# Stick-breaking attention issued one head ahead, and a vector-by-matrix product moved from VectorE to TensorE in four column groups

## The reference, cut to what matters

```python
def stick_breaking_attention(q, k, v):          # per head h of 8, dh = 64
    z = einsum('qd,kd->qk', q, k) * 64 ** -0.5
    neg_log_1m_beta = where(mask, softplus(z), 0.0)
    tail = cumsum(neg_log_1m_beta, reverse=True) - neg_log_1m_beta
    a = where(mask, exp(log_sigmoid(z) - tail), 0.0)
    return einsum('qk,kd->qd', a, v)

proj = rms_norm(x, g) @ w_in      # q k v | c_b c_c c_u | g_a g_b, 5120 columns
branch_a = stick_breaking_attention(q, k, v) @ w_sb
branch_b = short_conv_mixer(c_b, c_c, c_u, conv_w) @ w_conv
merged = sigmoid(g_a) * branch_a + sigmoid(g_b) * branch_b
x = x + merged @ w_out            # then router, experts, block two

# block two, needed there only
mod   = silu(c)     @ ada_w + ada_b     # ada_w is 1024 x 6144
mod_c = silu(c_ctx) @ ada_w + ada_b
```

## Time and profile before

| | us |
|---|---|
| median of 3 runs | 3600.28 (3599.87 to 3601.12) |
| the profiled execution, its own time | 3600.31 |
| its span | 3598.5 |
| the stretch of the list, from the first score matmul to the first matmul of the output projection | 130.0 to 528.4 |

### The profile page before, as it was taken

The page is one execution under the profiler, slowest core; times in us unless marked ns, Lnnn a source line. Parts: engine busy times, 40 slices in busy tenths (PEclk is TensorE's granted clock), DMA queues, the critical chain, the costliest instruction groups (busy, mean ns, idle before and its releaser), DMA issues.

```text
span 3598.5 us, 31608 instructions
## 1 busy us (share of the span) xinstructions
PE 3301.9 (92%) x12644; PEld 2110.6 (59%) x12644; DVE 1756.1 (49%) x3055; ACT 1020.0 (28%) x1262; POOL 271.8 (8%) x99
## 2 busy tenths in 40 slices
PE   7899887799977899999979999899999999999998
PEld 3344434444443344444448888677777777777776
DVE  2355482222214433233224888777635555555565
ACT  3524201121103210244023333455532222222222
POOL 0000000000000000000001433232300000000000
PEclk9999998799987999999989999999999999999999
DMA  5123252599970110110022333345454444444451
GB/s 188 47 100 110 95 186 72 201 341 364 366 284 5 47 47 0 70 47 24 24 86 102 131 133 141 135 182 199 179 202 152 152 152 152 144 148 142 174 187 47
DMA packets 270574, 500.01 MB, mean 139 GB/s; under 512 B 10103, under 2 KB 151543, under 8 KB 256920
## 3 DMA queue, kind: packets, MB, share of 16 engines
q1 hardware_dynamic: 239008, 391.67, 31.9%
q10 hardware_dynamic: 24648, 81.64, 5.6%
q0 software_dynamic: 6768, 24.64, 1.8%
HBM read 414.55 MB, written 83.36 MB: 138 GB/s over the span
## 4 chain that ended last, share of the span: by engine, by line
PE 77%; DVE 9%; ACT 8%; issue 4%; DMA 1%; ACTq 0%; DVEq 0%; POOL 0%; SPq 0%
PE P L1907 7%; PE P L1909 7%; PE P L1908 7%; PE P L1487 6%; PE P L1615 6%; PE P L1978 4%; PE P L1980 4%; PE P L1979 4%; PE P L1851 3%; PE P L1564 3%; PE P L1647 3%; PE P L1787 2%; DVE gin L402 2%; PE P L1537 2%; ACT part L1369 2%
## 5 line engine op out<-in xcount | busy, mean ns | idle before, releaser
L1907 PE MATMUL P<-hr,part 128*128 128x512 f32 x1152 | 459.4, 399 | 19.4 <-DVE part L402 19.4
L1908 PE MATMUL P<-hr,part 128*128 128x512 f32 x1152 | 456.0, 396 | 0.0
L1909 PE MATMUL P<-hr,part 128*128 128x512 f32 x1152 | 455.8, 396 | 0.0
L1978 PE MATMUL P<-ge,part 128*128 128x512 f32 x1024 | 402.4, 393 | 49.4 <-DVE y L402 45.5
L1980 PE MATMUL P<-ge,part 128*128 128x512 f32 x1024 | 400.5, 391 | 0.0
L1979 PE MATMUL P<-ge,part 128*128 128x512 f32 x1024 | 400.4, 391 | 0.0
L2026 POOL TENSOR_TENSOR part<-raw,part 128x2048 fp32r<-128x2048 f32 x48 | 230.1, 4795 | 1325.4 <-ACT part L1369 1325.4
L1369 ACT ACTIVATE part<-raw 128x2048 fp32r<-128x2048 f32 x136 | 260.2, 1914 | 190.3 <-PE P L1980 166.9
L402 DVE TENSOR_TENSOR part<-raw,part 128x2048 fp32r<-128x2048 f32 x88 | 201.5, 2291 | 154.5 <-ACT part L1369 154.5
L1487 PE MATMUL P<-H,W 128*128 128x512 f32 x576 | 256.4, 601 | 6.5 <-DVE H L410 6.5
L1907 PEld LDWEIGHTS P<-hr,part 128*128 128x128 f32 x1152 | 217.1, 188 | 71.0 <-DVE part L402 20.2
(11 more groups left out here) (258 smaller groups left out, 4040.7 us busy)
## 6 DMA issues: line engine op xcount, KB each, us to landing
raw<-in_u SPq DMA_DIRECT2D x64, 1024.0 KB, 4.9
raw<-in_v SPq DMA_DIRECT2D x64, 1024.0 KB, 5.3
W<-in_w_in SPq DMA_DIRECT2D x18, 2048.0 KB, 10.1
W<-in_w_gate SPq DMA_DIRECT2D x32, 1024.0 KB, 8.1
W<-in_w_up SPq DMA_DIRECT2D x32, 1024.0 KB, 12.6
W<-in_w_down SPq DMA_DIRECT2D x32, 1024.0 KB, 12.1
w_scratch<-window ACTq DMA_DIRECT2D x16, 2048.0 KB, 7.2
wr<-w_scratch SPq DMA_DIRECT2D x32, 1024.0 KB, 7.2
```

The source lines that it names most:

```text
L1907: t.matmul(bank[f % 3], wh[:, k, js], HR[0][:, k, :], start=k == 0, stop=False)
L1908: t.matmul(bank[f % 3], wh[:, k, js], HR[1][:, k, :], start=False, stop=False)
L1909: ins = t.matmul(bank[f % 3], wl[:, k, js], HR[0][:, k, :], start=False, stop=k == 7)
L1978: t.matmul(b, wh[:, k, js], gh[:, k, :], start=k == 0, stop=False)
```

## The change

Two edits, both to the list and to what its entries do.

**The order of the attention.** Phase 0 of head `h+1` is now issued ahead of phases 1 and 2 of head `h`. The rest (`pj 12..31` and the `ada` entries) is spread evenly between the 24 attention entries. The semaphore values, which were computed as `9 * h + ...`, now come from tables (`AX0`, `AA0`, `AV0`).

**The product with `ada_w`.** It has 13 entries instead of 49, and TensorE does the multiplying. The silu of both vectors is written into `SCP`, a 128x256 tile of zeros in which each group of 32 columns carries the two vectors in its first two columns. Entry `ada n` (n < 12) issues eight matmuls with a 128x32 stationary operand from `SCP` and a 128x512 part of `ada_w` as the moving one; part k goes to partitions 32*(k%4) to 32*(k%4)+31 of bank 6. ScalarE copies bank 6 to `ADR` (one 128x512 copy, part of the next `ada` entry), and four matmuls of 128x128 by 128x2 (against `SEL`, a pattern that picks rows 0 and 1 of every group of 32 and sums the groups) lay the result down in bank 7. VectorE has no part in any of this; after the list it adds the bias from bank 7 in one instruction. The `mg` steps have no `ada` entry between them any more.

```diff
+        SCP, SEL, ADR = ft[0][:, 0:256], ft[0][:, 256:288], ft[1]
...
-        att_steps = [("att", h, ph) for h in range(8) for ph in range(3)]
-        cv_steps = [("pj", p) for p in range(12, 32)]
-        both = []
-        while att_steps or cv_steps:
-            both += att_steps[:1] + cv_steps[:1]
-            del att_steps[:1], cv_steps[:1]
-        ada_steps = [("ada", i) for i in range(49)]
-        ORDER1 = interleave(both, ada_steps, 0.55)
-        ORDER1 += interleave([("pj", p) for p in range(32, 40)], ada_steps, 1)
-        ORDER1 += interleave([("mg", n) for n in range(16)], ada_steps, 1)
-        ORDER1 += ada_steps
+        att_steps = [("att", 0, 0)]
+        for h in range(8):
+            att_steps += ([("att", h + 1, 0)] if h < 7 else []) + [("att", h, 1), ("att", h, 2)]
+        beside = interleave([("pj", p) for p in range(12, 32)], [("ada", i) for i in range(13)], 0.6)
+        last_ada = [x for x in [("ada", i) for i in range(13)] if x not in beside]
+        ORDER1 = interleave(att_steps, beside, len(beside) / 23.0)
+        ORDER1 += beside
+        ORDER1 += interleave([("pj", p) for p in range(32, 40)], last_ada, 1)
+        ORDER1 += [("mg", n) for n in range(16)]
...
-            if kind == "ada" and i < 48 and i % 4 == 0:
-                slots.take(("ada", i // 4))
-            if kind == "ada" and i < 48 and i % 4 == 3:
-                slots.drop(("ada", i // 4), s["ada_v"], 10 * (i // 2) + 8)
+            if kind == "ada" and i < 12:
+                slots.take(("ada", i))
+                slots.drop(("ada", i), s["ada_mm"], max(1, 2 * i))
...
+            v.memset(SCP, 0.0).then_inc(s["z_v"], 1)
+            v.tensor_reduce(out=SEL, in_=ident.rearrange("p (g e) -> p e g", e=32), axis=AX.X, op=ADD).then_inc(s["z_v"], 1)
...
-            dve.wait_ge(s["ada_v"], 240)
-            tt(MOD, MOD, par("ab").unsqueeze(2).broadcast_to([128, 48, 2]), ADD).then_inc(s["ada_v"], 1)
+            dve.wait_ge(s["ada_mm"], 24)
+            tt(MOD, bank[7][:, 0:96].rearrange("p (k n) -> p k n", n=2), par("ab").unsqueeze(2).broadcast_to([128, 48, 2]), ADD).then_inc(s["ada_v"], 1)
...
+            act.wait_ge(s["z_v"], 2)
+            a.activation(SCP.rearrange("p (k n) -> p k n", n=32)[:, :, 0:2], par("cc").rearrange("p (k n) -> p k n", n=2), ACT.Silu).then_inc(s["sc_a"], 1)
             for kind, *i in ORDER1:
                 if kind == "att":
                     attention(*i)
+                elif kind == "ada" and i[0]:
+                    act.wait_ge(s["ada_mm"], 2 * i[0] - 1)
+                    a.activation(ADR, bank[6], ACT.Copy).then_inc(s["ada_a"], 1)
...
             def modulation(n):
-                if n and n % 2 == 0:
-                    u = n // 2 - 1
-                    pe.wait_ge(s["ada_v"], 10 * u + 8)
-                    t.matmul(bank[6], ones, ft[u % 2], start=True, stop=True).then_inc(s["ada_mm"], 1)
+                if n < 12:
+                    w = k8(slot["ada", n])
+                    pe.wait_ge(*full["ada", n])
+                    pe.wait_ge(s["sc_a"], 1)
+                    pe.wait_ge(s["ada_a"], n)
+                    for k in range(8):
+                        lo = 32 * (k % 4)
+                        ins = t.matmul(bank[6][lo:lo + 32, :], SCP[:, 32 * k:32 * k + 32], w[:, k, :], start=k < 4, stop=k >= 4)
+                    ins.then_inc(s["ada_mm"], 1)
+                if n:
+                    pe.wait_ge(s["z_v"], 3)
+                    pe.wait_ge(s["nv"], 33)
+                    pe.wait_ge(s["ada_a"], n)
+                    for c in range(4):
+                        at = 8 * (n - 1) + 2 * c
+                        ins = t.matmul(bank[7][:, at:at + 2], ADR[:, c * 128:(c + 1) * 128], SEL[:, 0:2], start=True, stop=True)
+                    ins.then_inc(s["ada_mm"], 1)
```

More of the change, by code:

```diff
@@ L207, in program @@
         H2 = tiles(38, 8)
-        att_steps = [("att", h, ph) for h in range(8) for ph in range(3)]
-        cv_steps = [("pj", p) for p in range(12, 32)]
-        both = []
-        while att_steps or cv_steps:
-            both += att_steps[:1] + cv_steps[:1]
-            del att_steps[:1], cv_steps[:1]
-        ada_steps = [("ada", i) for i in range(49)]
-        ORDER1 = interleave(both, ada_steps, 0.55)
-        ORDER1 += interleave([("pj", p) for p in range(32, 40)], ada_steps, 1)
-        ORDER1 += interleave([("mg", n) for n in range(16)], ada_steps, 1)
-        ORDER1 += ada_steps
+        att_steps = [("att", 0, 0)]
[7 more added lines that the diff above has]
+        ORDER1 += [("mg", n) for n in range(16)]
+        AX0, AA0, AV0, att_x = {}, {}, {}, []
+        na, nv_ = 0, 0
+        for _, h, ph in att_steps:
+            AX0[h, ph], AA0[h, ph], AV0[h, ph] = len(att_x), na, nv_
+            att_x += [(h, ph, i) for i in range(4 if ph < 2 else 1)]
+            na += (7, 1, 1)[ph]
+            nv_ += (5, 8, 0)[ph]
         pj_evac, n_act = [], 0
@@ L448, in attention @@
                         z = Z[:, OFF[i]:OFF[i] + n]
-                        b = bank[2 + (9 * h + 4 + i) % 4]
-                        dve.wait_ge(s["att_mm"], 9 * h + 5 + i)
+                        x = AX0[h, 1] + i
+                        b = bank[2 + x % 4]
+                        dve.wait_ge(s["att_mm"], x + 1)
                         tt(z, z, b[:, 0:n], SUB).then_inc(s["att_v"], 1)
-                        dve.wait_ge(s["att_v"], 13 * h + 6 + 2 * i)
+                        dve.wait_ge(s["att_v"], AV0[h, 1] + 2 * i + 1)
                         tt(z[:, 0:128], z[:, 0:128], cst("nmask"), ADD).then_inc(s["att_v"], 1)
@@ L468, in conv @@
                 tt(y, y, CB[:, c, :], MUL).then_inc(s["cv"], 1)
-            eye = ident.unsqueeze(1).broadcast_to([128, 4, 128])
-            def modulation(n):
-                if n and n % 2 == 0:
-                    u = n // 2 - 1
[L475 to L495, removed]
             def merge(n, ga, gb, mm, done, gates):
@@ L1151, in attention @@
                         n = 512 - 128 * i
[L1152 removed]
+                        x = AX0[h, 0] + i
+                        act.wait_ge(s["att_mm"], x + 1)
                         if h >= 2:
[L1154 to L1156 removed]
+                            act.wait_ge(s["att_mm"], AX0[h - 2, 2] + 1)
+                        a.activation(Z[:, OFF[i]:OFF[i] + n], bank[2 + x % 4][:, 0:n], ACT.Copy, scale=0.125).then_inc(s["att_a"], 1)
+                    act.wait_ge(s["att_a"], AA0[h, 0] + 4)
                     a.activation(E, Z, ACT.Abs).then_inc(s["att_a"], 1)
[L1158 removed]
+                    act.wait_ge(s["att_a"], AA0[h, 0] + 5)
                     a.activation(E, E, ACT.Exp, scale=-1.0).then_inc(s["att_a"], 1)
[L1160 removed]
+                    act.wait_ge(s["att_a"], AA0[h, 0] + 6)
                     a.activation(E, E, ACT.Ln, bias=1.0).then_inc(s["att_a"], 1)
                 if ph == 1:
[L1163 removed]
+                    act.wait_ge(s["att_v"], AV0[h, 1] + 8)
                     a.activation(Z, Z, ACT.Exp).then_inc(s["att_a"], 1)
                 if ph == 2:
[L1166 to L1167 removed]
+                    x = AX0[h, 2]
+                    act.wait_ge(s["att_mm"], x + 1)
+                    a.activation(AT[po:po + 64, j, :], bank[2 + x % 4][po:po + 64, :], ACT.Copy).then_inc(s["att_a"], 1)
             act.wait_ge(s["zd"], 16 * (NT - 32))
[L1170 removed]
+            act.wait_ge(s["z_v"], 2)
+            a.activation(SCP.rearrange("p (k n) -> p k n", n=32)[:, :, 0:2], par("cc").rearrange("p (k n) -> p k n", n=2), ACT.Silu).then_inc(s["sc_a"], 1)
             for kind, *i in ORDER1:
@@ L1572, in tensor_program @@
             pe.wait_ge(s["h_v"], 16)
-            pe.wait_ge(s["ada_v"], 239)
+            pe.wait_ge(s["ada_v"], 1)
             for q in range(4):
```

26 lines of the change are left out of this document (12 added, 14 removed).

## The result

The changed kernel takes 3615.33 us (median of 6 runs, 3612.43 to 3618.75), the kernel before 3600.7 us beside it (3598.55 to 3601.18). The ratio is 1.0043 with a 95% interval of 1.003 to 1.0056: slower, by 15 us. The forecast was slower by 40. The profiled execution has a span of 3612.8 us, 14.3 more than before.

A forecast was written before the change was run, and what follows sets the result against it. It took TensorE, then a VectorE-bound tail, to limit a 398.4 us stretch; TensorE work, added waits, half clock and gating summed to 438 us, 39.6 longer, giving 3640 us (own range 3622 to 3656; 8 in 10: 3603 to 3681).

The forecast's parts named there:

- What bounds the kernel before: Attention to output projection, 398.4 us: TensorE nearly always busy until 448 us, then a VectorE-bound tail of 80.3 us.
- the last gating: VectorE work left at the end of the mg steps after the change: about 2 us.
- The price of an entry: Eight column-group matmuls on TensorE overlap in pairs: 3.87 us an entry, 46.4 in all, between bounds of 1.72 and 6.87.
- the four groups overlap in full: Rival for the ada_w product on TensorE: 20.6 us in place of 46.4, giving 3614 us, still slower; chance 0.18.
- The added wait: TensorE waits at ada entries for ScalarE's late-queued copy of bank 6: 46 us in twelve places, at most 8 each.
- The half clock behind the waits: TensorE runs at its lower clock after seven waits over 3 us: 1.7 us each, 12 us in all.
- The small matmuls: Four matmuls after each copy of bank 6: 0.87 us an entry, 10.4 us over twelve entries.
- Loads, ScalarE's copies as work, preparation: Loading ada_w pieces, 7 us of ScalarE copying, and memset, reduction and silu: put at no added time.
- The rival on the faster side: ScalarE copies bank 6 before TensorE's next entry, so waits and half clock vanish: 380 us stretch, 3582 us; chance 0.11.
- That the phases are not hidden: Rival in the attention: two heads share banks 2 to 5, so phase 1 waits for copies; adds 0 to 15 us.

The follow-up runs named there:

- e3: The kernel before with only the attention phases issued one head ahead, the product staying on VectorE: 3578.79 us, ratio 0.9947.
- e4: The changed kernel with ScalarE's copy of bank 6 moved right behind its matmuls, and the attention in the old order: 3597.0 us, ratio 1.0001.
- g3: The changed kernel with parts 0 and 1 in the first column group, 2 and 3 in the second and so on: 3616.75 us, ratio 1.0048.
- f2: The early copy with attention by pairs of heads, in phase 2 one head's four matmuls ahead of the other's: 3554.52 us, ratio 0.9874.
- early copy: The changed kernel with ScalarE's copy of bank 6 moved from entry n+1 to entry n, right behind its matmuls: 3556.54 us, ratio 0.9885.
- f3: The early copy run again unchanged, on another chip: 3555.87 us, ratio 0.9881 to the kernel before.
- f1: The early copy with attention by pairs of heads, the phase 2 matmuls of both heads issued in turn: 3547.72 us, ratio 0.9857.

## Why the prediction was wrong

The direction was right, the time was not: 3640 forecast, 3615 measured. That is below the forecast's own range of 3622 to 3656, and inside the wide range that was to hold it 8 times in 10, from 3603 on. Step by step:

**What bounds the kernel before: right.** The tail bound by VectorE went (80.3 us to 54.9 of `mg` steps; the 2 us for the last gating did not show), and the waits between phase 0 and phase 1 too. e3 and e4 confirm both from the other side.

**The price of an entry: the step that failed.** The term "nine slots of 0.43 us for 16 records: 3.87 us an entry, 46.4 in all" measured 1.92 us, 23.0 in all. This is 23.4 us of the 25 by which the forecast missed; the smaller misses below nearly cancel. I had the price between bounds of 1.72 and 6.87, and chose the middle by a mechanism, "if matmuls start in program order", that no row bore out. The 1.92 us of after and the 1.95 of g3 show its fault: each group works through its own matmuls, and a record whose group is busy does not stop the following ones as long as no more than three of one group are waiting, as far as g3 and f2 show. The Trainium skill says of tiles, on the page "TensorEngine Tiling (Array Packing)", Key Properties, that different ones can load weights and multiply in parallel; the traces here agree, with 3.7 times the speed in four groups (7.03 / 1.92). The Trainium skill's sentence in "TensorE: Matmul & The Clock Gate", Part 3, that matmuls start and end in strict program order does not fit the records of g3, whose thirteenth started in the first round, and an entry of 1.95 us. The rival "the four groups overlap in full" gave 3614 us: it was the right case, with 0.18. That it came within 2 us of the measured time is luck in part: its 20.6 us for the product are 2.4 too low, the waits 5.2 and the gating 2 too high.

**The added wait: right in place, mechanism and size.** Forecast 46 us in twelve places, at most 8 each. Measured 39.6 us in eleven places, longest 7.5, and 1.2 more ahead of the last small matmuls. By kind of place it is 19.8 us behind phase 0 (forecast 20.2), 14.3 behind phase 1 (16.4) and the rest, 6.6, behind phase 2 or a projection step (7.0). The early copy removes all of it. This decided the sign, as the prediction said, and no price of the product between the two bounds would have turned it: close to the lower one the change was still slower.

**The half clock behind the waits: right in the sum, by luck in part.** Forecast 12 us, as 1.7 for each of seven waits over 3 us. From the chain of after: twelve entries of column-group matmuls come to 30.8 us where 12 x 1.92 is 23.0, the small ones to 13.6 where 12 x 0.98 is 11.8, phase 1 at 185.79 took 6.08 instead of 4.44, and the projection step at 233.80 took 8.50 instead of 6.97. Sum 12.8 us. There were seven such waits, but only five of them had half-clock work behind them, at 1.7 to 4.2 us each. Three waits were alike, 3.16 us behind phase 1: the entry behind the first took 2.89 us at a granted clock of 0.64, those behind the other two 1.92 at 1.00.

```profile
229.11:232.00 2.89, 2.89 (x17) 0.65 (x17) 0.00 (x0) 0.00 (x0) 0.00 (x0) 0.64 0.00 0
385.36:387.28 1.92, 1.92 (x17) 0.53 (x17) 0.00 (x0) 1.16 (x1) 0.00 (x0) 1.00 0.03 9
```

So a price per wait is a mean at best.

**The small matmuls:** forecast 0.87 an entry, measured 0.98 at the full clock, 11.8 in all against 10.4. **Loads, ScalarE's copies as work, preparation:** put at nothing, and no row shows a cost.

**The account with measured terms:** 192.4 + 73.8 + 54.9 + 23.0 + 11.8 + 40.8 + 12.8 = 409.5 us, where 412.3 were measured.

**The rival on the faster side** named the right lever: without the wait and its clock the kernel would be faster. With the measured price its sum is 380 less 23.4, 357 us for the stretch, and the early copy took 356.1. What was wrong with it as a rival is that in the changed kernel the copy is not early.

**That the phases are not hidden** (banks shared by two heads): not seen, no wait of this kind in after or in the early copy.

## What to carry to other kernels

When work moves to another engine, look where its result is picked up: an instruction queued in the place of its consumer, behind other work, makes the producer wait even if both engines have time, and moving the pick-up behind its producer was worth some 57 us here (a ratio of 1.0043 to one of 0.9885). Narrow stationary operands paid here only when spread over several column groups (7.03 us an entry in one, 1.92 in four); issue the groups in turn, since a long run of one group closes the overlap (eight records in f2; four, in g3, did not). Price a term that no row shows by its two bounds, and let a rule that would halve the gain count no more than one that would not.

## What the hardware showed that I had not expected

Float32 matmuls with 32 columns overlap four deep with little loss: 16 records in 1.92 us against 7.03 in one group, with both records of a matmul in the same group. With 64 columns two overlap, 2.30 us for two heads against 4.60. The order of issue hardly matters over four records of a group (1.95 against 1.92 us) and does over eight (3.86 against 2.30). What closes the overlap in f2 is the run of records for one group: the second head's first record started right behind the first head's fifth of eight, in all four pairs.

In after, the 16 records took 3.60 to 3.64 us behind waits of 4.9 to 7.5 us, 2.89 behind one wait of 3.16 and 1.92 behind two others of the same length, and 1.92 behind waits of 1.4. The lower level also came with no wait ahead of it. The early copy, run again (f3), has a projection step of 8.51 us where its neighbours take 7.06, at a granted clock of 0.52; ahead of it TensorE was busy without a gap, with column-group, small and score matmuls:

```profile
319.25 1.85 PE P L1524 x16
321.10 0.98 PE P L1532 x8
322.09 2.55 PE P L1500 x8
324.63 8.51 PE P L1475 x16
```

f1 and f2 have one such step each, of 8.76 us, and the first trace of the early copy has none in this stretch. What brings it on stays open; one such step costs 1.5 to 1.7 us.
